# Token-major chunk data laid out by pair parity, PE transposes instead of identity products, and state and carried terms added on VectorE

## The chip, the cores and the metric

The kernel runs on 1 core of one Trainium2 chip. The metric is the device time of one execution, in microseconds (us); smaller is better. The median of three runs of the kernel before is 1719.84 us (1719.4 to 1721.35).

## What is computed

One step of a two-layer encoder trunk, for 64 tokens of a running stream and 512 tokens of a new one: 576 tokens, 9 chunks of 64. Per layer:

```
proj = RMSNorm(x) @ w_in                       # (576, 1024) @ (1024, 3344)
GLA group, 4 heads, 64 keys x 128 values, per chunk:
    scores = tril(q_e @ k_e^T);  o = scores @ v + q_e @ s
    s      = s * exp(last) + (k * exp(last - cum))^T @ v
RWKV-7 group, 8 heads of 64, per token:
    sa = s @ a;  s = s*w + outer(sa, b) + outer(v, k);  y = s @ r
x = x + [norm(o)*silu(g) | groupnorm(y)*g] @ w_out
x = x + ConvFFN(RMSNorm(x))                    # 1024 -> 2 x 2816 -> 1024
```

All in float32. The matmuls of the large projections run as three passes over operands split in two (high and low part, `fp32r`); those of the chunked recurrences are plain float32 products. The state of chunk 0 comes from the inputs, chunk 1 starts a new stream with a zero state, chunks 2 to 8 follow it.

## The kernel before, in words

Every engine has a program written out by hand, and semaphores join them. A list per engine (`PE_F`, `AC_B`, `DV_G` and so on, lines 106 to 132) names the events in the order in which the engine signals them, and a wait names an event of a chunk. So the order of the work is the order of the calls in each engine's loop, and nothing is rescheduled.

A layer has these stages: the projections (`dense`, L591 and L592), the chunked recurrences (the **scan stage**, L749 to L1088 on TensorE), the output projection and the ConvFFN. The change touches the scan stage alone. In it features lie on partitions: the 8 RWKV heads are 4 pairs `p`, with an even head on partitions 0 to 63 and an odd one on 64 to 127. X = A, B is a group of two pairs, `q` is the pair in its group, `hp` the head in its pair.

The loop `for i in range(-1, LAST)` (L998) does in one **step** the front of chunk j = i + 1 and the back of chunk i:

- `gram` (L760): per group 8 products with 128 columns (L770) and 4 with 64 (L773), of the chunk's keys and queries, into `gr[X]` and `tk[X]`. VectorE masks them (`mask_inverse` L1842, `mask_gram` L1852).
- `tokens` (L777): turns the three token-major operands (64 tokens on partitions), 12 products with `ident2` per group (L783). ScalarE copies them out (`copy_tokens`, L1335, 384 columns).
- `level` k = 1 to 5 (L787): powers and product of the triangular inverse. After each, ScalarE copies the powers (`copy_powers`, L1341), VectorE adds the product (`add_power`, L1859).
- `solve_z`, `solve_z1`, `solve_z2`, `solve_u` (L822 to L864): four products in a row with a copy between them: Z and Z1 go out on ScalarE (`copy_back`, L1350), W on VectorE (`add_rest`, L1871), U on ScalarE. `solve_z` accumulates the product with the state (L838) in PSUM.
- `outputs` (L866): y (L874, L877, L879) and the new state (L883, L886, L888), where L886 adds the old state as an identity product. VectorE scales the state (`new_state`, L1876), ScalarE copies y.
- `gla_scores`, `gla_tokens`, `gla_out`, `gla_state` (L897 to L950): the same for GLA; L949 adds the old state as an identity product.
- `post_means`, `post_squares_o`, `post_squares_y` (L957 to L986): at i = 0, 2, 4, 6, 7 the means for the normalisations; their logarithms and exponentials on ScalarE (L1386, L1392, L1398, L1404), scaling on VectorE (`scale_o` L1910, `scale_y` L1917).

Chunk 8's back stands after the loop (L1062 to L1085), and the output projection follows. In these products each head uses its own quarter of the PE array: an even head reads partitions 0 to 63 and writes 0 to 63, an odd one 64 to 127 both. Consecutive products alternate between these two tiles of 64x64:

```python
for p, h, q in heads(X):            # L782: h is the head's half of the partitions
    mm = e.matmul(tk[X][h, (2 * a + q) * C:(2 * a + q + 1) * C], src[h, p, :], ident2[h, :], ...)
```

Of the kernel before, what the change touches and what calls it, by code (L numbers as in the profile page):

```python
# [105 lines left out]
PE_F = ["gramA", "gramB", "tokA", "L1A", "tokB", "L1B", "L2A", "L2B", "L3A", "L3B", "L4A", "L4B", "L5A", "L5B"]  # L106
AC_F = ["tokA", "L1A", "tokB", "L1B", "L2A", "L2B", "L3A", "L3B", "L4A", "L4B"]
DV_F = ["EA", "DA", "EB", "DB", "MA", "MB", "L2A", "L2B", "L3A", "L3B", "L4A", "L4B", "L5A", "L5B"]
PO_F = ["TA", "TB"]

PE_B = ["Z", "Z1", "Z2", "U", "Y", "S"]
AC_B = ["Z", "Z1", "U", "Y"]
DV_B = ["W", "St"]
# [3 lines left out]
DV_G = ["scm", "Sg"]  # L117
# [17 lines left out]
def program(nc, x_prompt, x_sample, state_gla, state_rwkv, state_rwkv_shift, cache_ffn_conv,  # L135
# [4 lines left out]
    with ExitStack() as ctx:  # L140
# [66 lines left out]
        EK = [cut([P, NP, 2, P]) for _ in range(2)]  # L207
# [3 lines left out]
        Z, Z1, W, U = (cut([P, NP, C]) for _ in range(4))  # L211
        St = cut([P, NP, C])
        Sg = cut([P, 2, GDV])
        Sraw = cut([P, NP, C])
# [39 lines left out]
        zb, ys, gb, pb = bank(4), bank(5), bank(6), bank(7)  # L254
# [6 lines left out]
        def by_half(ap):  # L261
            return ap.rearrange("p (b t) -> p b t", t=HT)

# [200 lines left out]
        def _(po):  # L464
# [62 lines left out]
            for l in range(0, DEPTH):  # L527
# [10 lines left out]
                def start_inverse(j):  # L538

                    n = l * NCH + j  # L540
                    for X, N in ((0, "A"), (1, "B")):
                        po.wait_ge(dv_f, nth(DV_F, n, "E" + N))
                        e.tensor_tensor(DET[1][:, X, :, 1, :], DET[0][:, X, :, 0, :],
                                        ident2[:, :].unsqueeze(1).broadcast_to([P, 2, C]), ALU.add).then_inc(po_f, 1)
# [41 lines left out]
        def _(pe):  # L586
# [65 lines left out]
            for l in range(0, DEPTH):  # L652
# [96 lines left out]
                def heads(X):  # L749

                    for q in range(2):
                        for hp in range(2):
                            yield 2 * X + q, slice(64 * hp, 64 * hp + 64), q
# [6 lines left out]
                def gram(j, X):  # L760

                    N, cc = "AB"[X], bass.ds(j * C, C)
                    if j > 0:
                        front(dv_f, DV_F, j - 1, "L5" + N)
                    for q in range(2):
                        p = 2 * X + q
                        for b, src in ((0, KA[:, p, cc]), (1, R[:, 4 + p, cc])):
                            for hp in range(2):
                                h = slice(64 * hp, 64 * hp + 64)
                                e.matmul(gr[X][h, (2 * q + b) * P:(2 * q + b + 1) * P], src[h],  # L770
                                         RW[h, p:p + RT + 1:RT, cc], start=True, stop=True)
                    for p, h, q in heads(X):
                        mm = e.matmul(tk[X][h, 384 + q * C:384 + (q + 1) * C], KK[h, p, cc], KA[h, p, cc],  # L773
                                      start=True, stop=True)
                    mm.then_inc(pe_f, 1)

                def tokens(j, X):  # L777

                    cc = bass.ds(j * C, C)
                    front(dv_f, DV_F, j, "D" + "AB"[X])  # L780
                    for a, src in enumerate((KA[:, :, cc], R[:, 4:8, cc], R[:, 8:12, cc])):
                        for p, h, q in heads(X):  # L782
                            mm = e.matmul(tk[X][h, (2 * a + q) * C:(2 * a + q + 1) * C], src[h, p, :], ident2[h, :],  # L783
                                          start=True, stop=True)
                    mm.then_inc(pe_f, 1)

                def level(j, X, k):  # L787

                    N, d = "AB"[X], DET[(k + 1) % 2]
                    powers = gr[X][:, 0:4 * C].rearrange("p (q c t) -> p q c t", q=2, c=2)  # L790
                    product = pair3(tk[X][:, 0:2 * C])
# [8 lines left out]
                    for q in range(2):  # L800
                        for hp in range(2):
                            h = slice(64 * hp, 64 * hp + 64)
                            if k < 4:
                                mm = e.matmul(powers[h, q, 0], d[h, X, q, 2], d[h, X, q, 0], start=True, stop=True)  # L804
                        for hp in range(2):
                            h = slice(64 * hp, 64 * hp + 64)
                            if k < 5:
                                mm = e.matmul(powers[h, q, 1], d[h, X, q, 0], d[h, X, q, 2], start=True, stop=True)  # L808
                        for hp in range(2):
                            h = slice(64 * hp, 64 * hp + 64)  # L810
                            if k > 1:
                                mm = e.matmul(product[h, q], d[h, X, q, 2], d[h, X, q, 1], start=True, stop=True)  # L812
                    mm.then_inc(pe_f, 1)

                HEADS = (slice(0, C), slice(C, 2 * C))

                def pairs(out):

                    for p in range(NP):
                        yield p, p // 2, p % 2, out[:, p * C:(p + 1) * C]  # L820

                def solve_z(i):  # L822

                    cc = bass.ds(i * C, C)
                    front(ac_f, AC_F, i, "tokB")
                    front(dv_f, DV_F, i, "MB")
                    glas(ac_g, AC_G, i, "oE")
# [4 lines left out]
                    for p, X, q, o in pairs(zb):  # L832
                        for h in HEADS:
                            mm = e.matmul(o[h], EK[i % 2][h, p, 1, C:2 * C], tok[i % 2][h, X, 2, q, :],
                                          start=True, stop=i == 1)
                        if i != 1:
                            for h in HEADS:
                                mm = e.matmul(o[h], KK[h, p, cc], St[h, p, :], start=False, stop=True)  # L838
                    mm.then_inc(pe_b, 1)

                def solve_z1(i):

                    back(ac_b, AC_B, i, "Z")
                    front(dv_f, DV_F, i, "L5B")
                    for p, X, q, o in pairs(zb[:, 256:512]):
                        for h in HEADS:
                            mm = e.matmul(o[h], Tf[i % 2][h, p, :], Z[h, p, :], start=True, stop=True)  # L847
                    mm.then_inc(pe_b, 1)

                def solve_z2(i):  # L850

                    back(ac_b, AC_B, i, "Z1")
                    for p, X, q, o in pairs(zb):
                        for h in HEADS:
                            mm = e.matmul(o[h], EK[i % 2][h, p, 0, C:2 * C], Z1[h, p, :], start=True, stop=True)
                    mm.then_inc(pe_b, 1)

                def solve_u(i):

                    back(dv_b, DV_B, i, "W")  # L860
                    for p, X, q, o in pairs(zb[:, 256:512]):
                        for h in HEADS:
                            mm = e.matmul(o[h], Tf[i % 2][h, p, :], W[h, p, :], start=True, stop=True)  # L863
                    mm.then_inc(pe_b, 1)  # L864

                def outputs(i):  # L866

                    cc = bass.ds(i * C, C)
                    back(ac_b, AC_B, i, "U")
                    if i > 0:  # L870
                        back(ac_b, AC_B, i - 1, "Y")
                    for p, X, q, o in pairs(ys):
                        for h in HEADS:
                            e.matmul(o[h], tok[i % 2][h, X, 2, q, :], EK[i % 2][h, p, 1, 0:C], start=True, stop=False)  # L874
                        if i != 1:
                            for h in HEADS:
                                e.matmul(o[h], St[h, p, :], R[h, p, cc], start=False, stop=False)  # L877
                        for h in HEADS:
                            mm = e.matmul(o[h], U[h, p, :], EK[i % 2][h, p, 0, 0:C], start=False, stop=True)  # L879
                    mm.then_inc(pe_b, 1)  # L880
                    for p, X, q, o in pairs(ys[:, 256:512]):
                        for h in HEADS:
                            e.matmul(o[h], tok[i % 2][h, X, 1, q, :], tok[i % 2][h, X, 2, q, :], start=True, stop=False)  # L883
                        if i != 1:
                            for h in HEADS:
                                e.matmul(o[h], ident2[h, :], St[h, p, :], start=False, stop=False)  # L886
                        for h in HEADS:
                            mm = e.matmul(o[h], tok[i % 2][h, X, 0, q, :], U[h, p, :], start=False, stop=True)  # L888
# [8 lines left out]
                def gla_scores(j):  # L897

                    cc = bass.ds(j * C, C)
                    if j > 0:  # L900
                        glas(dv_g, DV_G, j - 1, "Sg")
# [18 lines left out]
                def gla_out(j):  # L920
# [3 lines left out]
                    if j > 0:  # L924
                        back(ac_b, AC_B, j - 1, "U")
# [13 lines left out]
                def gla_state(j):  # L939

                    glas(ac_g, AC_G, j, "oO")
                    for q in range(2):
                        o = gb[:, q * GDV:(q + 1) * GDV]
                        for h in HEADS:
                            mm = e.matmul(o[h], gtok[h, 256 + q * C:256 + (q + 1) * C], gtok[h, q * GDV:(q + 1) * GDV],
                                          start=True, stop=j == 1)
                        if j != 1:
                            for h in HEADS:
                                mm = e.matmul(o[h], ident2[h, :], Sg[h, q, :], start=False, stop=True)  # L949
# [7 lines left out]
                def post_means(g):  # L957
# [3 lines left out]
                    back(ac_b, AC_B, sum(GROUPS[g]) - 1, "Y")  # L961
# [1165 lines left out]
```

## Time and profile before

| | us |
|---|---|
| median of 3 runs | 1719.84 |
| the profiled execution, its own time | 1718.78 |
| its span | 1716.9 |
| PE busy | 1683.0 (98%), 19077 matmul records |
| DVE, ACT, POOL busy | 910.2, 665.4, 558.5 |
| scan stage, layer 0 and 1 | about 209.7 to 388.7 and 1050.2 to 1229 |

A plain float32 matmul leaves two load records and two matmul records in the trace, an `fp32r` one and a transpose one of each. A form such as "64*64 64x128" tells the rows and columns of the array that are used, then the moving operand. The end of a matmul is modelled, so a row's duration is latency; the pace is read from the starts of successive rows. The granted clock of TensorE is 0.997 of full speed over the span and 1.00 in the stages of the change.

### The profile page before, as it was taken

Reading aid. Unit: us, or ns where it says so; the run is one execution under the profiler, and the core shown is the slowest. Engines: PE = TensorE matmul, PEld = TensorE weight load, DVE = VectorE, ACT = ScalarE, POOL = GpSimd, SP = SyncE. Lnnn points to the kernel's source line nnn. Section 1 sums busy time; section 2 is a strip of 40 time slices with the busy share of each in tenths; the row PEclk is TensorE's granted clock in tenths of the full one; section 3 lists DMA queues with packets and bytes.
Section 4 is the critical chain, followed back from the end, with each engine's and each line's share of the span. In section 5 each row is a group of like instructions: output and inputs, shape, how many; then the busy total and the mean of one; then the engine's idle time right before and its main releaser. Section 6 shows DMA issues by size and latency. Waiting matters only on the chain.

```text
span 1716.9 us, 42320 instructions
## 1 busy us (share of the span) xinstructions
PE 1683.0 (98%) x19077; PEld 1626.7 (95%) x19077; DVE 910.2 (53%) x1382; ACT 665.4 (39%) x1017; POOL 558.5 (33%) x293
## 2 busy tenths in 40 slices
PE   7999999989999999999999999999899999999997
PEld 7999999879999999999999999998799999999997
DVE  4669534345566504666546883344456662166643
ACT  5444344554433212333343533454534331133323
POOL 5443301112343433334333432012134434343431
PEclk9999999999999999999999999999999999999999
DMA  5223200002222322223322222000022232222331
GB/s 147 63 74 84 69 24 4 4 3 68 76 85 86 98 76 75 87 86 96 83 75 74 74 74 58 10 4 3 20 83 79 86 96 85 71 83 87 92 94 56
DMA packets 218869, 115.51 MB, mean 67 GB/s; under 512 B 9332, under 2 KB 216450, under 8 KB 218690
## 3 DMA queue, kind: packets, MB, share of 16 engines
q1 hardware_dynamic: 218610, 112.79, 22.9%
q8 instruction: 151, 2.47, 0.6%
q14 instruction: 28, 0.23, 0.0%
q10 hardware_dynamic: 80, 0.02, 0.0%
HBM read 109.27 MB, written 3.53 MB: 66 GB/s over the span
## 4 chain that ended last, share of the span: by engine, by line
PE 95%; ACT 3%; DVE 1%; issue 0%; POOL 0%; DMA 0%; DVEq 0%; ACTq 0%
PE ps L591 37%; PE ps L592 37%; PE ps L808 2%; PE ps L812 2%; PE ps L770 2%; PE ps L804 1%; PE ps L783 1%; PE ps L596 1%; PE ps L914 1%; PE ps L874 1%; PE ps L977 1%; PE ps L706 1%; PE ps L931 1%; PE ps L863 1%; PE ps L847 0%; PE ps L888 0%
## 5 line engine op out<-in xcount | busy, mean ns | idle before, releaser
L518 POOL TENSOR_TENSOR wlo<-raw,whi 128x1024 fp32r<-128x1024 f32 (+1 forms) x188 | 508.7, 2706 | 865.1 <-ACT whi L1149 865.0
L1149 ACT ACTIVATE whi<-raw 128x1024 fp32r<-128x1024 f32 (+1 forms) x188 | 209.5, 1114 | 650.0 <-PE ps L592 650.0
L591 PE MATMUL ps<-xh,whi 128*128 128x288 f32 x1120 | 332.9, 297 | 4.2 <-DVE xl L1565 4.2
L592 PE MATMUL ps<-xh,whi 128*128 128x288 f32 x1120 | 331.2, 296 | 0.0
L591 PE MATMUL ps<-xl,whi 128*128 128x288 f32 x1120 | 330.3, 295 | 0.0
L592 PE MATMUL ps<-xl,whi 128*128 128x288 f32 x1120 | 329.0, 294 | 0.0
L591 PE MATMUL ps<-xh,wlo 128*128 128x288 f32 x1120 | 328.8, 294 | 0.0
L592 PE MATMUL ps<-xh,wlo 128*128 128x288 f32 x1120 | 328.7, 294 | 0.0
L591 PEld LDWEIGHTS ps<-xh,whi 128*128 128x128 f32 x1120 | 210.5, 188 | 6.3 <-issue 4.7
L592 PEld LDWEIGHTS ps<-xh,whi 128*128 128x128 f32 x1120 | 210.6, 188 | 0.2
L591 PEld LDWEIGHTS ps<-xh,wlo 128*128 128x128 f32 x1120 | 210.7, 188 | 0.0
L592 PEld LDWEIGHTS ps<-xl,whi 128*128 128x128 f32 x1120 | 210.6, 188 | 0.0
L591 PEld LDWEIGHTS ps<-xl,whi 128*128 128x128 f32 x1120 | 210.1, 188 | 0.0
L592 PEld LDWEIGHTS ps<-xh,wlo 128*128 128x128 f32 x1120 | 209.9, 187 | 0.0
L2035 DVE TENSOR_TENSOR x<-x,ps 128x576 f32<-128x576 f32 x48 | 36.2, 754 | 197.2 <-PE ps L592 197.2
L2073 DVE SCALAR_TENSOR_TENSOR cv<-up,par,cv 128x578 f32<-128x578 f32 x44 | 100.5, 2284 | 32.8 <-ACT cv L1521 32.8
L2088 DVE SCALAR_TENSOR_TENSOR hl<-hf,hh 128x576 fp32r<-128x576 f32 x44 | 98.4, 2237 | 33.3 <-ACT hh L1527 33.3
L592 PE MATMUL ps<-hh,whi 128*128 128x288 f32 x352 | 103.7, 295 | 0.0
L592 PE MATMUL ps<-hl,whi 128*128 128x288 f32 x352 | 103.6, 294 | 0.0
L591 PE MATMUL ps<-hl,whi 128*128 128x288 f32 x352 | 103.5, 294 | 0.0
L591 PE MATMUL ps<-hh,wlo 128*128 128x288 f32 x352 | 103.4, 294 | 0.0
L591 PE MATMUL ps<-hh,whi 128*128 128x288 f32 x352 | 103.4, 294 | 0.0
(294 smaller groups left out, 3286.7 us busy)
## 6 DMA issues: line engine op xcount, KB each, us to landing
raw<-in_ffn_w_up SPq DMA_DIRECT2D x88, 512.0 KB, 3.8
raw<-in_w_in SPq DMA_DIRECT2D x52, 512.0 KB, 3.7
raw<-in_ffn_w_down SPq DMA_DIRECT2D x32, 704.0 KB, 4.5
raw<-in_w_out SPq DMA_DIRECT2D x16, 512.0 KB, 3.6
xin<-in_x_prompt SPq DMA_DIRECT2D x4, 512.0 KB, 6.3
out<-xin SPq DMA_DIRECT2D x8, 256.0 KB, 2.9
out<-RW SPq DMA_DIRECT2D x16, 64.0 KB, 2.2
g<-in_rwkv_g SPq DMA_DIRECT2D x2, 256.0 KB, 3.0
```

The lines of the kernel that those rows point to most:

```text
L518: e.tensor_tensor(wlo[s][:, 0:width], raw[s][:, 0:width], whi[s][:, 0:width].bitcast(F32), ALU.subtract).then_inc(w_lo[s], 1)
L591: e.matmul(acc(out)[:, 0], lhsT, rhs[:, 0:HT], start=start, stop=stop)
L592: return e.matmul(acc(out)[:, 1], lhsT, rhs[:, HT:TOK], start=start, stop=stop)
L596: e.matmul(out[:, 0:512], lhsT, rhs[:, 0:512], start=True, stop=True)
L706: ws = e.matmul(PS[2][:, tt], w2a2[0:64, p * P:(p + 1) * P], R[0:64, 12, tt], start=True, stop=True)
L770: e.matmul(gr[X][h, (2 * q + b) * P:(2 * q + b + 1) * P], src[h], RW[h, p:p + RT + 1:RT, cc], start=True, stop=True)
L808: mm = e.matmul(powers[h, q, 1], d[h, X, q, 0], d[h, X, q, 2], start=True, stop=True)
L812: mm = e.matmul(product[h, q], d[h, X, q, 2], d[h, X, q, 1], start=True, stop=True)
L1149: e.activation(whi[s][:, 0:width], raw[s][:, 0:width], ACT.Copy).then_inc(w_hi[s], 1)
L2035: e.tensor_tensor(by_half(xt), by_half(xt), acc(PS[s]), ALU.add).then_inc(psum_free[s], 1)
L2073: e.scalar_tensor_tensor(out=cv[:, :], in0=up[:, 1:3 + TOK], scalar=par[:, cw + FF + f:cw + FF + f + 1], in1=cv[:, :], op0=ALU.mult, op1=A ...
L2088: e.scalar_tensor_tensor(out=hl[:, it, :], in0=hf[:, :], scalar=1.0, in1=hh[:, it, :].bitcast(F32), op0=ALU.mult, op1=ALU.subtract).then_i ...
```

## The change

Per chunk, the token-major data of a pair now lies on the partition half given by the parity of the pair (q), while the head parity (hp) picks the column block. `gram`, the product with the state (now `carried`) and `outputs` therefore read from one half and write to the other for half of their products: they use all four 64x64 tiles. `tokens` becomes 12 transposes of whole pairs, alternately 128 and 64 columns wide. The identity products of the states go. VectorE adds the old states, the carried part of Z and the carried part of y; ScalarE copies the two carried parts out of PSUM (`Zc`, `Yc`), VectorE writes Z and y in ScalarE's place. Both groups of a chunk are handled by one `gram`, one `tokens`, one copy of 768 columns. In the loop, `solve_z2` comes after `gla_scores` and the means, `solve_u` after both first levels, `outputs` after both second levels; ScalarE's `square_o` moves from the end of a step to the start of the next.

```diff
+                def gram(j):
...
                     if j > 0:
-                        front(dv_f, DV_F, j - 1, "L5" + N)
...
+                        front(dv_f, DV_F, j - 1, "L5B")
+                    if j > 0 and j != 2:
+                        back(ac_b, AC_B, j - 1, "Zc")
+                    for X in range(2):
+                        for b in range(2):
+                            at = (2 * X + b) * P
+                            for hp, q, p, own, tok_half in all_four(X):
+                                src = R[own, 4 + p, cc] if b else KA[own, p, cc]
+                                e.matmul(gr[hp][tok_half, at:at + P], src, RW[own, p:p + RT + 1:RT, cc], start=True, stop=True)
+                        for hp, q, p, own, tok_half in all_four(X):
+                            mm = e.matmul(tk[hp][tok_half, 384 + X * C:384 + (X + 1) * C], KK[own, p, cc], KA[own, p, cc],
...
+                def tokens(j):
...
+                    for a, first in enumerate((RT + NP, 4, 8)):
+                        for X in range(2):
+                            at, even, odd = a * P, first + 2 * X, first + 2 * X + 1
+                            e.transpose(tk[X][:, at:at + P], rows[:, bass.ds(odd * TOK + j * C - C, P)], ident[:, :])
+                            mm = e.transpose(tk[X][0:C, at:at + P], RW[:, even, cc], ident[:, :])
...
                         if k == 2:
                             front(po_f, PO_F, j, "T" + N)
+                            front(ac_f, AC_F, j, "tok")
...
+                def carried(i):
...
+                    front(ac_f, AC_F, i, "L4B")
...
+                        for hp, q, p, own, tok_half in all_four(X):
+                            mm = e.matmul(gr[hp][tok_half, X * C:(X + 1) * C], KK[own, p, cc], St[own, p, :],
...
+                def carried_y(i):
...
+                    glas(dv_g, DV_G, i, "Sa")
...
+                            mm = e.matmul(gb[h, p * C:(p + 1) * C], St[h, p, :], R[h, p, cc], start=True, stop=True)
...
                 def solve_z1(i):
 
-                    back(ac_b, AC_B, i, "Z")
+                    back(dv_b, DV_B, i, "Z")
...
                 def outputs(i):
...
+                    for X in range(2):
+                        for hp, q, p, own, tok_half in all_four(X):
+                            e.matmul(out_banks[own, q, X * C:(X + 1) * C], tok[i % 2][tok_half, X, 2, hp, :],
+                                     EK[i % 2][tok_half, hp, X, 1, 0:C], start=True, stop=False)
...
-                        if i != 1:
-                            for h in HEADS:
-                                e.matmul(o[h], ident2[h, :], St[h, p, :], start=False, stop=False)
...
-                        if j != 1:
-                            for h in HEADS:
-                                mm = e.matmul(o[h], ident2[h, :], Sg[h, q, :], start=False, stop=True)
...
+                def add_z(i):
+
+                    step(pe_b, PE_B, i, "Z")
...
+                        step(ac_b, AC_B, i, "Zc")
+                        e.tensor_tensor(Z[:, :, :], Zc[:, :, :], pair3(zb[:, 0:256]), ALU.add).then_inc(dv_b, 1)
...
+                        e.tensor_tensor(y, by_pair(Yc), from_rows(0), ALU.add).then_inc(dv_b, 1)
...
+                        e.tensor_tensor(by_pair(St), by_pair(St), from_rows(2 * C), ALU.add).then_inc(dv_b, 1)
+                        step(dv_b, DV_B, i, "Sa")
+                        e.tensor_tensor(St[:, :, :], St[:, :, :], decay, ALU.mult).then_inc(dv_b, 1)
...
                 scale_y(N_Y - 1)
+                add_z(LAST)
                 add_rest(LAST)
```

The last hunks are VectorE's: `add_z`, `add_y`, `new_state` (`new_gla_state` changes in the same way) and its order after the loop. In its loop the order is now `add_z(i)`, `mask_inverse(j)`, `mask_gram(j, 0)`, `mask_gram(j, 1)`, `add_rest(i)`, and `new_state(i)`, `add_y(i)` follow the adds of level 2. For chunk 1, whose state is zero, nothing is carried.

`all_four(X)` yields, for hp and q in 0, 1, the pair p = 2X + q, its rows `own` = half hp and the half `tok_half` = half q.

## Rows read from the trace of the kernel before

**Rows 1.** The page: the chain that ended last, by engine.

```profile
PE 95%; ACT 3%; DVE 1%; issue 0%; POOL 0%; DMA 0%; DVEq 0%; ACTq 0%
```

**Rows 2.** Busy time in layer 0's scan stage: window, us, PE, PEld, DVE, ACT, POOL, clock, DMA.

```profile
209.70:385.70 176.00, 170.71 (x4535) 155.89 (x4534) 71.67 (x204) 88.00 (x203) 21.14 (x29) 1.00 0.05 12
```

**Rows 3.** Groups of instructions by line, PE: form, records, busy us, mean ns, idle before.

```profile
L770 PE MATMUL ps<-RW 64*64 64x128 f32 x576 | 37.8, 270 | 0.0
L783 PE MATMUL ps<-ident,RW 64*64 64x64 f32 x864 | 32.0, 219 | 0.0
...
L883 PE MATMUL ps<-work 64*64 64x64 f32 x288 | 20.1, 218 | 0.0
...
L886 PE MATMUL ps<-work,ident 64*64 64x64 f32 x256 | 18.1, 218 | 0.0
...
L838 PE MATMUL ps<-work,RW 64*64 64x64 f32 x256 | 15.8, 218 | 0.0
...
L773 PE MATMUL ps<-RW 64*64 64x64 f32 x288 | 14.5, 218 | 0.0
...
L949 PE MATMUL ps<-work,ident 64*64 64x128 f32 x128 | 12.3, 269 | 0.0
```

**Rows 4.** Timeline of PE in the step i = 2: start us, latency us, line, records.

```profile
257.68 1.04 PE L770 MATMUL ps<-RW 64*64 64x128 f32 x16
258.55 0.40 PE L773 MATMUL ps<-RW 64*64 64x64 f32 x8
258.78 0.63 PE L847 MATMUL ps<-work 64*64 64x64 f32 x16
...
269.92 0.28 PE L812 MATMUL ps<-work 64*64 64x64 f32 x4
270.13 0.66 PE L914 MATMUL ps<-ident,G 128*64 128x128 f32 x8
270.72 0.45 PE L916 MATMUL ps<-ident,G 64*64 64x64 f32 x8
```

**Rows 5.** Timeline of PE where it transposes, between projections.

```profile
798.87 0.27 PE L1114 MATMUL ps<-ident,last_rows 128*28 128x128 f32 x1
798.98 0.27 PE L1115 MATMUL ps<-ident,last_conv 128*88 128x128 f32 x1
...
1691.33 1.91 PE L643 MATMUL ps<-ident,work 128*128 128x128 f32 x16
1693.00 0.38 PE L591 MATMUL ps<-hh,whi 128*128 128x288 f32 x1
```

**Rows 6.** Timeline of PE, products from the two halves of the partitions.

```profile
49.24 0.69 PE L706 MATMUL ps<-RW,w2a 64*128 64x512 f32 x1
49.24 0.69 PE L707 MATMUL ps<-RW,w2a 64*128 64x512 f32 x1
49.77 0.59 PE L706 MATMUL ps<-RW,w2a 64*128 64x512 f32 x1
```

**Rows 7.** Timeline of ACT and DVE from step i = 4 to 5; last, a group by line.

```profile
316.69 0.36 ACT L1353 ACTIVATE work<-ps 128x256 f32<-128x256 f32 x1
...
316.97 2.17 DVE L1922 SCALAR_TENSOR_TENSOR RW<-RW,par,work 128x128 f32<-128x128 f32 x4
319.06 0.28 DVE L1847 TENSOR_TENSOR work<-ps,m_be 128x128 f32<-128x128 f32 x1
...
L1338 ACT ACTIVATE work<-ps 128x384 f32<-128x384 f32 x18 | 8.8, 491 | 26.0 <-PE ps L783 26.0
```

**Rows 8.** Timeline of PE and DVE after the loop, layer 0; idle before in brackets.

```profile
377.76 0.68 PE L847 MATMUL ps<-work 64*64 64x64 f32 x16
...
378.93 0.68 PE L855 MATMUL ps<-work 64*64 64x64 f32 x16 [0.48 <-ACT work L1353]
...
380.32 0.41 DVE L1874 TENSOR_TENSOR work<-work,ps 128x256 f32<-128x256 f32 x1
...
380.78 0.68 PE L863 MATMUL ps<-work 64*64 64x64 f32 x16 [1.17 <-DVE work L1874]
```

More of the change, by code:

```diff
@@ L205, in cut @@
                                    **dict(zip(names[1:], sizes[1:])))
[L207 removed]
+        EK = [cut([P, 2, 2, 2, P]) for _ in range(2)]
         tok = [cut([P, 2, 3, 2, C]) for _ in range(2)]
@@ L211, in program @@
         Z, Z1, W, U = (cut([P, NP, C]) for _ in range(4))
+        Sraw = W
+        Zc, Yc = (cut([P, NP, C]) for _ in range(2))
         St = cut([P, NP, C])
         Sg = cut([P, 2, GDV])
-        Sraw = cut([P, NP, C])
         gtok = cut([P, 2 * GDV + 2 * C])
@@ L758, in _ @@
                 back = glas = front
-                def gram(j, X):
-                    N, cc = "AB"[X], bass.ds(j * C, C)
+                def gram(j):
+                    cc = bass.ds(j * C, C)
                     if j > 0:
-                        front(dv_f, DV_F, j - 1, "L5" + N)
[L765 to L775, printed above, removed]
@@ L792, in level @@
+                def level(j, hp, k):
+                    N, d = "AB"[hp], DET[(k + 1) % 2]
+                    powers = gr[hp][:, 0:4 * C].rearrange("p (x c t) -> p x c t", x=2, c=2)
+                    product = pair3(tk[hp][:, 0:2 * C])
                     if k == 1:
@@ new lines, in solve_z @@
+                def solve_z(i):
+                    front(ac_f, AC_F, i, "tok")
+                    front(dv_f, DV_F, i, "MB")
+                    glas(ac_g, AC_G, i, "oE")
+                    if i > 0:
+                        back(dv_b, DV_B, i - 1, "Y")
+                    for n, hp, X, o in solved(zb):
+                        for h in HEADS:
+                            mm = e.matmul(o[h], EK[i % 2][h, hp, X, 1, C:2 * C], tok[i % 2][h, X, 2, hp, :],
+                                          start=True, stop=True)
+                    mm.then_inc(pe_b, 2 if i == 1 else 1)
@@ L1063, in _ @@
                 squares = SQ[:, 0, :].rearrange("p (a t) -> p a t", t=2 * C)
+                carried(LAST)
                 solve_z(LAST)
-                back(ac_b, AC_B, LAST - 1, "Y")
-                glas(dv_g, DV_G, LAST, "Sg")
-                chunk_mean(7, gb[:, 0:256], R[:, 0:4, seventh])
+                front(dv_f, DV_F, LAST, "L5A")
+                back(dv_b, DV_B, LAST - 1, "Y")
+                chunk_mean(7, bank(2)[:, 0:256], R[:, 0:4, seventh])
+                carried_y(LAST)
                 solve_z1(LAST)
@@ L1975, in _ @@
                         add_power(j, 1, k)
+                        if k == 2 and i >= 0:
+                            new_state(i)
+                            add_y(i)
                     if i == LAST - 1:
@@ L2007, in _ @@
                 new_state(LAST)
+                add_y(LAST)
                 cc = group(N_Y)[1]
```

289 lines of the change are left out of this document (156 added, 133 removed).

## The prediction

> **What bounds the kernel now.** First the chain of waits: TensorE holds 95% of it [rows 1]. Then the busy time of the scan stage, the only one that the change touches: PE is busy for 170.7 of 176.0 us at the full clock of 2.4 GHz, ACT for 88, DVE for 72 [rows 2]. So a product that leaves PE shortens the stage, as long as ScalarE and VectorE deliver in time. Last the pace of PE, from starts. Eight products of 128 columns (16 records, L770) take 258.55 - 257.68 = 0.87 us, 0.218 for a pair; four of 64 columns (L773) take 0.23, 0.117 for a pair [rows 4]. A "pair" is what now shares the array: an even head and an odd one. There are 18 chunks (9 in each layer); a float32 product is two records.
>
> **What leaves PE.** `tokens` loses all of L783: 864 records, 216 pairs, x 0.117 = 25.2 us. The identity products of the RWKV state (L886) are 256 records, 64 pairs, 7.5 us; those of the GLA state (L949) 128 records, 32 pairs x 0.218 = 7.0 us [rows 3, 4].
>
> **What comes: the transposes.** 12 x 18 = 216. Sixteen of them started within 1693.00 - 1691.33 = 1.67 us, 0.104 each, and one after another of another width 0.11 later [rows 5]. I take 0.11, for the narrow ones too, since there 28 columns cost no less: 23.8 us. They use all 128 rows, the products around them 64. Such an excursion has a row: L914 starts 0.21 after the last L812 group, 0.09 more than its pace, and its four products take 0.59 where two pairs take 0.44, 0.15 more [rows 4]. That makes 0.24; I take 0.34, as an estimate for wide loads, x 18 = 6.1 us. So the "one-pass" transposes save nothing: 29.9 us for 25.2, +4.7. The balance of PE so far is -14.5 + 4.7 = -9.8 us.
>
> **What may shrink: the crossed products.** `gram`, `carried` and `outputs` keep their counts, but reach all four 64x64 tiles, in the order (rows 0, columns 0), (0, 1), (1, 0), (1, 1) or likewise. Does the array run four at once? No row has four 64x64 tiles; two rows bound it. L914 runs two products on all rows into different columns: four of them, 128 columns each, in 0.59 us, where one at a time they would need 4 x 0.218 = 0.87 [rows 4]. L706 and L707 read different halves of the rows into the same columns, start together and follow each other every 0.53 us with 512 columns [rows 6], so they overlap too. The change also puts the two row halves into different banks of PSUM, as L706 and L707 do. If both overlaps combine, four take the time of two. Half of L770 (144 pairs x 0.218 = 31.4) is 15.7 us; half of L773, L838 and the four lines of `outputs` like L883 (72 + 64 + 288 = 424 pairs x 0.117 = 49.6) is 24.8 us [rows 3, 4]. The bounds are 0 and 40.5 us; below 0 if products from the same rows don't overlap (a rival). I take 40.5, since each of the two overlaps has its row. PE: -50.3 us.
>
> The Trainium skill, "TensorEngine Tiling (Array Packing)", sections on tiling modes and restrictions, speaks for this: 64x64 mode has four independent tiles, and row tiles need different banks. No trace here shows all four.
>
> **What comes back as waits**, per layer, with durations of [rows 7, 8] and the paces above, found by laying out the calls of the four engines' loops in their written order, one after the other, before and after the change; PE comes earlier to nearly every wait.
> - z1 to z2: from the last z1 product through ScalarE's copy to z2 took 0.70 us, 0.48 of it idle [rows 8]. `gram` of group B lay between them; now `gla_scores` alone does (0.23), and the means where there are any. Chunks 0, 1, 3, 5: 4 x 0.41 = 1.6 us.
> - `add_z` stands before z1 and `gram` is short: three waits of about 0.4, 1.2 us.
> - After steps 2, 4 and 6: ScalarE is in its logarithms and exponentials and reaches the copy of Z at 316.69 only [rows 7]. Before, the first half of `gram` ran meanwhile; now `gram` itself waits for that copy (`Zc` reads its banks): 1.3 + 1.7 + 1.7. VectorE's scaling of y ends at 319.06, where the masks start [rows 7]; `add_z` queues behind it, and z1 waits 1.2 + 1.0 + 1.0 more. Less the 0.8 of waits that are there today: 7.0 us. This is the largest term.
> - Chunk 0: the transposes wait for both masks (0.8), level 2 for the copy of 768 columns (0.5; 384 take 0.49 and 256 take 0.36 [rows 7], so about 0.85), less what goes: 1.3 us.
> - After the loop, `add_z(LAST)` stands behind four scalings, so at 380.3 [rows 8], where z1 started at 377.76: z1 waits 3.5, z2 and u 0.6 each, the means of chunk 8 1.5 (three VectorE operations where there was one and a copy), with 0.4 more in small waits; today's waits there are 4.1. So +2.6 us.
>
> Sum 13.7 per layer, 27.4 for both. The copies of Yc, the second state operation and `add_y` (about 0.4 us each on an engine that is busy for 41%) lie beside `gla_tokens` and level 3, over 1.5 us of PE; their cover gone, they would cost 1.2 us a chunk. POOL's start of the inverse waits for one mask of both groups, 0.15 us later, long before level 2. SP's queue and the DMAs are not passed by anything that moves.
>
> **Sum**: -50.3 + 27.4 = -22.9 us. The profiled execution took 1718.8, 1.1 below the median; 1719.8 - 22.9 = **1697 us**. Own range of this case 1688 to 1706: the waits may be 18 to 36 us.
>
> **Rivals.**
> - *PE is fed no faster.* Today's best pace is one record in 29 ns (0.23 us for 8, L773 [rows 4]). If that is the sequencer's limit, four passes of 64 columns need 0.117, as now, and only `gram`'s 128 columns gain: -9.8 - 15.7 = -25.5, waits +21: 1715 us. Against it: 0.117 also is what a pair's array time asks for. Chance 0.17.
> - *Two at a time.* The crossed tiles only pair. PE -9.8, and with `gram` at full length fewer waits, about 17: 1727 us. Against it stand both rows above. Chance 0.17.
> - *The transposes pay for each change of width* (the other side, with its place and price). They alternate 128 and 64 columns, 11 changes within a chunk, 198 in all. A change between 64*64 and 128*64 costs 0.09 + 0.15, so 0.12 to 0.24 each way [rows 4]; at 0.18, 36 us: 1733 us. It decides from 0.116 us a change (22.9 / 198). Against it: L1114 (28 columns) to L1115 (88) took 0.11, the pace without any change [rows 5]. Chance 0.12.
> - *Products from the same rows don't overlap*: the crossed ones take twice as long, 1719.8 - 9.8 + 81 + 14 = 1805 us; L914 speaks against it. Chance 0.03.
>
> The Trainium skill, same page, "Key Properties", says that a change of tiling mode drains TensorE, and its restrictions bar transposes of float32 from column tiling; by that the third rival's 1733 us would come out. The trace agrees for 64*64 to 128*64, not for L1114 to L1115.
> For the first rival, "TensorE: Matmul & The Clock Gate", Part 1, gives 25 ns as the smallest distance of two starts; four passes of 64 columns would then need 100 ns, a seventh of 49.6 us would go, and an estimate by that page is 1709 us. No trace here shows it.
>
> **Numbers.** Forecast 0.47, rivals 0.17, 0.17, 0.12, 0.03; 0.04 is left for a mixture. About 0.2% (3.4 us) can be told from no change: faster is below 1716.4, slower above 1723.3. Faster: 0.47 + 0.12 of the first rival + 0.03: 0.62. Same: 0.05 of the first, 0.04 of the second, 0.02: 0.11. Slower: 0.27. Range 1690 to 1737: it takes in three of the cases and leaves out the fourth rival, some of the third and the low end of the forecast.
>
> **What would show it.** Four records of L770's successor starting within some 20 ns and `gram` at some 1.1 us instead of 2.2; transposes 0.11 apart whatever their width; after steps 2, 4, 6 PE waiting for ScalarE's copy of Zc, then for `add_z`; after the loop z1 waiting 3 us or more for VectorE. If `gram` still takes over 2 us, the forecast is wrong by its main term; if the 12 transposes take over 2.5 us, by the second.

## The result: about half of the forecast gain, and the profile after

The kernel after takes **1708.48 us** by the median of four runs (1708.15 to 1712.2), the kernel before, beside it, 1719.99. The ratio is 0.9937 (95% interval 0.992 to 0.9954): faster by 11.5 us, by more than the 3.4 us that can be told from no change. Forecast was 1697 us, 22.9 less. The sign is right and the wide range (1690 to 1737) holds the time, but half of the gain is missing, and the forecast's own range, 1688 to 1706, is missed by 2.5 us.

| | before | after |
|---|---|---|
| profiled execution, us | 1718.78 | 1708.42 |
| its span, us | 1716.9 | 1706.6 |
| granted clock over the span | 0.997 | 0.987 |
| scan stage, layer 0 / 1, us | 179.5 / 179.5 | 172.8 / 175.2 |
| matmul records | 19077 | 18045 |

The page of the kernel after, busy time and the chain by engine, answers to [rows 1]:

```profile
PE 1650.7 (97%) x18045; PEld 1583.9 (93%) x18045; DVE 932.9 (55%) x1414; ACT 659.0 (39%) x995; POOL 557.7 (33%) x293
...
PE 92%; ACT 3%; DVE 3%; issue 1%; DMA 1%; POOL 0%; SPq 0%; DVEq 0%; ACTq 0%
```

TensorE still holds the chain, VectorE has gone from 1 to 3%. From here on a scan stage is measured from the first product of `gram` to the last of `turn_state`, which turns the final state. Busy time in such windows has the columns of [rows 2]. First the kernel before, both layers:

```profile
209.66:389.16 179.50, 173.32 (x4560) 157.88 (x4560) 73.65 (x210) 91.19 (x208) 21.14 (x29) 1.00 0.05 12
1049.54:1229.04 179.50, 173.32 (x4560) 157.88 (x4560) 73.60 (x210) 91.20 (x208) 21.14 (x29) 1.00 0.05 12
```

Then the kernel after, both layers, and five short stretches inside them:

```profile
210.26:383.05 172.79, 155.34 (x4044) 135.24 (x4044) 84.95 (x226) 87.84 (x197) 20.99 (x29) 0.96 0.05 12
1043.42:1218.65 175.23, 157.43 (x4043) 137.00 (x4044) 85.53 (x226) 87.82 (x197) 20.96 (x29) 0.94 0.05 12
...
303.60:310.40 6.80, 4.94 (x160) 4.63 (x158) 4.23 (x10) 4.55 (x10) 1.27 (x1) 1.00 0.01 2
310.40:317.20 6.80, 5.93 (x63) 5.04 (x64) 3.24 (x9) 0.87 (x2) 3.27 (x4) 0.50 0.01 2
317.20:324.00 6.80, 6.80 (x234) 6.49 (x232) 2.34 (x7) 3.50 (x9) 0.00 (x0) 1.00 0.02 5
371.80:378.60 6.80, 5.80 (x106) 4.65 (x110) 2.32 (x4) 3.35 (x6) 0.00 (x0) 0.50 0.01 2
...
1204.70:1218.30 13.60, 10.05 (x128) 7.89 (x130) 7.14 (x19) 4.36 (x9) 0.00 (x0) 0.50 0.00 1
```

Two things are to be seen. Both layers do the same work, before in the same time, after in times 2.4 us apart. And the clock column, 1.00 before, is 0.96 and 0.94: for 6.8 us in step i = 5, for 6.8 us after the loop of layer 0 and for 13.6 us at the end of layer 1 TensorE is granted half its clock, 1.2 instead of 2.4 GHz. (Two more of 3.4 us each lie in layer 1, at about 1109 and 1146.6.) No step of the forecast has this. The page's row of tenths over 40 slices doesn't show it: it says 9 nearly throughout.

**The four tiles** do what was forecast. The timeline of PE, DVE and ACT in the kernel after, from step i = 4 to 5 (start us, latency us):

```profile
308.38 0.36 ACT L1386 ACTIVATE work<-ps 128x256 f32<-128x256 f32 x1
...
308.65 2.17 DVE L1999 SCALAR_TENSOR_TENSOR RW<-RW,par,work 128x128 f32<-128x128 f32 x4
...
308.89 0.67 PE L784 MATMUL ps<-RW 64*64 64x128 f32 x16 [1.68 <-ACT work L1386]
...
309.35 0.32 PE L786 MATMUL ps<-RW 64*64 64x64 f32 x8
...
309.46 0.65 PE L784 MATMUL ps<-RW 64*64 64x128 f32 x16
...
309.90 0.32 PE L786 MATMUL ps<-RW 64*64 64x64 f32 x8
...
310.75 0.41 DVE L1919 TENSOR_TENSOR work<-work,ps 128x256 f32<-128x256 f32 x1
...
311.21 1.12 PE L878 MATMUL ps<-work 64*64 64x64 f32 x16 [0.99 <-DVE work L1919]
```

Sixteen records of 128 columns now take 0.46 us (308.89 to 309.35) and eight of 64 columns 0.11, where one group took 0.87 and 0.23 [rows 4]. The whole `gram` takes 1.1 us. The lines around them are the two waits that were forecast: `gram` waits 1.68 us for the copy of Z (`Zc`, L1386), z1 (L878) then 0.99 us for `add_z` (L1919), which stands behind four scalings (L1999).

**The transposes** keep one pace whatever their width: 0.17 us after the first, then 0.11 from start to start. PE of the kernel after, one chunk:

```profile
228.02 0.33 PE L797 MATMUL ps<-ident,RW 128*128 128x128 f32 x1
228.19 0.27 PE L798 MATMUL ps<-ident,RW 128*64 128x128 f32 x1
228.30 0.27 PE L797 MATMUL ps<-ident,RW 128*128 128x128 f32 x1
...
229.28 0.27 PE L798 MATMUL ps<-ident,RW 128*64 128x128 f32 x1
229.48 0.33 PE L818 MATMUL ps<-work 64*64 64x64 f32 x4
```

**After the loop**, layer 0, kernel after, what answers to [rows 8]:

```profile
371.26 0.41 DVE L1919 TENSOR_TENSOR work<-work,ps 128x256 f32<-128x256 f32 x1
...
371.73 1.08 PE L878 MATMUL ps<-work 64*64 64x64 f32 x16 [2.94 <-DVE work L1919]
...
373.29 1.12 PE L886 MATMUL ps<-work 64*64 64x64 f32 x16 [0.48 <-ACT work L1398]
...
374.93 1.12 PE L894 MATMUL ps<-work 64*64 64x64 f32 x16 [0.53 <-DVE work L1935]
```

z1 waits 2.94 us. And its own sixteen records last 1.08 us where the same shape took 0.68 before [rows 8]: this is at half clock (0.50 in the window 371.80 to 378.60 above).

### The profile page after: what moved, and what is told of

It is laid out like the page before. It is cut to its first block, busy times and chain, and to the rows that moved or that the text cites. A ratio compares the mean times of both kernels' runs of the same rounds, so it can differ in the third digit from the quotient of the medians.

```text
span 1706.6 us, 40374 instructions
## 1 busy us (share of the span) xinstructions
PE 1650.7 (97%) x18045; PEld 1583.9 (93%) x18045; DVE 932.9 (55%) x1414; ACT 659.0 (39%) x995; POOL 557.7 (33%) x293
## 4 chain that ended last, share of the span: by engine, by line
PE 92%; ACT 3%; DVE 3%; issue 1%; DMA 1%; POOL 0%; SPq 0%; DVEq 0%; ACTq 0%
PE ps L601 37%; PE ps L602 37%; PE ps L821 2%; PE ps L818 2%; PE ps L824 2%; PE ps L606 1%; PE ps L797 1%; PE ps L886 1%; DVE RW L1999 1%; PE ps L878 1%; ACT L1443 1%; PE ps L798 1%; PE ps L942 1%; PE ps L1003 1%; PE ps L894 1%
## 5 line engine op out<-in xcount | busy, mean ns | idle before, releaser
L1910 DVE TENSOR_TENSOR work<-work,ps 128x128 f32<-128x128 f32 x144 | 39.6, 286 | 123.0 <-PE ps L824 123.0
L602 PE MATMUL ps<-hh,whi 128*128 128x288 f32 x352 | 103.7, 295 | 0.0
```

The lines of the kernel that those rows point to most:

```text
L602: return e.matmul(acc(out)[:, 1], lhsT, rhs[:, HT:TOK], start=start, stop=stop)
L1910: e.tensor_tensor(dst, DET[(k + 1) % 2][:, X, :, 1, :], src, ALU.add).then_inc(dv_f, 1)
```

## The experiments

The theory, A: the forecast of the instructions and waits holds, and what is missing is the clock. TensorE's granted clock falls to half behind the new waits, and the stretches at half cost some 11 us. The rival, B: the waits alone cost more than laid out, and the clock changes nothing that bounds. Each kernel ran beside the kernel before on the same chip. In the table "gain" is the median of before less that of the kernel; clock is that of the profiled execution over its whole span.

| kernel | median us | ratio to before (95%) | gain | clock |
|---|---|---|---|---|
| after | 1708.48 | 0.9937 (0.992 to 0.9954) | 11.5 | 0.987 |
| after, again | 1708.2 | 0.9923 (0.991 to 0.9936) | 12.2 | 0.988 |
| waits filled | 1699.13 | 0.987 (0.9856 to 0.9883) | 21.6 | 0.996 |
| last wait filled | 1704.48 | 0.9898 (0.9881 to 0.9914) | 16.2 | 0.998 |
| filled twice over | 1710.07 | 0.9939 (0.9926 to 0.9953) | 10.3 | 0.996 |
| order in the loop | 1696.54 | 0.9864 (0.9849 to 0.9879) | 23.8 | 0.992 |
| order after the loop | 1706.18 | 0.9906 (0.989 to 0.9922) | 14.5 | 0.991 |
| both orders | 1692.02 | 0.9836 (0.9823 to 0.9849) | 28.9 | 0.992 |
| two tiles | 1729.3 | 1.0052 (1.0037 to 1.0067) | -8.4 | 0.987 |
| crossed identity products | 1695.41 | 0.9854 (0.9837 to 0.9871) | 25.5 | 0.988 |
| crossed, both orders | 1681.8 | 0.977 (0.9754 to 0.9785) | 38.9 | 0.991 |
| the same, waits filled | 1678.9 | 0.9756 (0.9743 to 0.9769) | 41.5 | 0.996 |

**Work for nothing in the waits.** The added products go into a bank that is free then, and nothing reads them. If A holds, added work makes the kernel faster.

```diff
+FILL = {3: (2, 2), 5: (3, 2), 7: (3, 2)}
...
+                def fill(i, n):
+                    t = tok[i % 2]
+                    for k in range(n):
+                        for h in HEADS:
+                            e.matmul(out_banks[h, 1, 0:256], t[h, 0, 0, 0, :], t[h, 0, 0:2], start=True, stop=True)
...
+                    if i in FILL:
+                        fill(i, FILL[i][0])
                     gram(j)
+                    if i in FILL:
+                        fill(i, FILL[i][1])
...
                 carried_y(LAST)
+                fill(LAST, 6)
                 solve_z1(LAST)
```

> The kernel after, plus work for nothing in the waits of the scan: pairs of 64x64 products of 256 columns into the free second bank of the outputs (0.107 us a pair at the full clock), two or three pairs before the crossed products and two before z1 in steps 3, 5 and 7, six pairs after the loop before z1. That is 20 pairs a layer, 4.3 us of added TensorE work in both layers, nothing taken away. Theory A (the forecast's missing half is the clock: behind the new waits TensorE's granted clock falls to half in the scan stages, which costs some 12 us): fewer half-clock stretches in the scan, and the time falls to 1697 to 1704 although work was added. Theory B (the new waits themselves are longer than forecast, the clock changes nothing that bounds): the time stays at 1708.5 or rises by up to 4.3 us, to 1713.

Measured 1699.13 us, in A's range and 9.3 below the kernel after. Its timeline of PE in front of `gram` of step i = 5, and the two scan stages:

```profile
309.70 1.49 PE L865 MATMUL ps<-work 64*64 64x256 f32 x12
311.54 0.67 PE L785 MATMUL ps<-RW 64*64 64x128 f32 x16 [0.34 <-ACT work L1399]
...
211.98:380.85 168.87, 159.73 (x4125) 136.60 (x4124) 85.12 (x226) 87.87 (x197) 21.03 (x29) 1.00 0.05 13
1041.25:1210.36 169.11, 159.68 (x4124) 136.37 (x4124) 84.97 (x226) 87.87 (x197) 21.03 (x29) 1.00 0.05 13
```

The clock is 1.00 in both stages, and they are 3.9 and 6.1 us shorter than in the kernel after, with the same products, the same waits for the same events and 160 records more. B, by which the clock is worth nothing, allowed no gain at all: it falls. One number of the expectation was wrong. A product of 256 columns is two records that follow each other every 0.1 us (the starts of 12 records fill about 309.70 to 310.8), so a pair costs 0.4 us, not 0.107, and the added work was some 16 us for both layers. It was nearly hidden because the waits had room for its 8 us a layer. From the start of the last record before each wait to the start of the first one behind it they are 1.47 + 1.13 + 1.90 + 1.21 + 1.90 + 1.21 + 3.16 = 12.0 us.

**Only the wait after the loop filled** (the last `fill` alone).

> Only the six pairs of products for nothing after the loop, before z1 (0.64 us a layer at the full clock, inside the wait of 3.16 us). Theory A (the clock falls behind the waits after the loop and stays at half through z2, u and the last outputs): less of the half-clock stretch after the loop, 1703 to 1707. Theory B (that stretch waits for ScalarE and VectorE, so TensorE's clock is worth nothing there): 1708 to 1709.

Measured 1704.48 us (1699.14 to 1705.95), in A's range. The profiled execution was one of the two fast ones, 1700.90 us. It has no half-clock stretch in either scan stage, though the waits within the loop are the same to 0.1 us, so for the loop the edit can't be the reason. It therefore shows the stage of the kernel after at full clock:

```profile
212.31:380.47 168.16, 152.84 (x4069) 132.49 (x4068) 84.98 (x226) 87.87 (x197) 21.00 (x29) 1.00 0.05 13
1040.87:1211.11 170.24, 153.76 (x4069) 133.00 (x4068) 85.04 (x226) 87.88 (x197) 21.01 (x29) 1.00 0.05 13
```

Layer 1 has one gap of about 1.5 us inside `gram` of step i = 0 that the kernel after doesn't have and that nothing here explains.

**The control**, the kernel after once more.

> The kernel after, unchanged, once more, as the control beside the others of this group. 1708 to 1711 by the median. Theory A (the clock's falls behind the waits come and go from one execution to the next): single executions differ by several us, down to 1703, and the half-clock stretches lie elsewhere than in the first profile, while the waits themselves are the same to 0.1 us. Theory B (the waits alone): executions within 2 us of each other and the same steps long.

Measured 1708.2 us by the median, single executions from 1704.13 to 1710.15. The half-clock stretches lie in part elsewhere: within layer 0's loop the first profile has one from 310.4 to 317.2 us, this one two of 3.4 us, at 310.6 and at 348.1. In layer 1 the one at 1109 stays and the one at 1146.6 is gone. The waits are the same in both (1.68 us for `gram`, 0.99 for z1 in step i = 5). So one step can be compared with itself. Windows of step i = 5, where the three kernels have the same instructions and waits. First the kernel after:

```profile
308.89:327.20 18.31, 17.26 (x441) 15.84 (x442) 9.06 (x25) 6.80 (x18) 4.54 (x5) 0.81 0.01 4
1144.29:1161.33 17.04, 15.99 (x441) 14.90 (x443) 8.95 (x25) 6.70 (x18) 4.53 (x5) 0.90 0.02 5
```

The control:

```profile
308.20:325.49 17.29, 16.25 (x441) 15.15 (x444) 8.98 (x25) 6.70 (x18) 4.54 (x5) 0.90 0.02 4
1144.14:1160.04 15.90, 14.66 (x443) 13.74 (x445) 8.96 (x25) 6.70 (x18) 4.55 (x5) 1.00 0.02 5
```

The kernel with only the last wait filled:

```profile
310.78:326.61 15.83, 14.58 (x442) 13.67 (x444) 8.98 (x25) 6.71 (x18) 4.56 (x5) 1.00 0.01 3
```

The step's length goes by the clock column alone: 15.8 to 15.9 us at 1.00, 17.0 to 17.3 with 3.4 us at half, 18.3 with 6.8 us. A microsecond at half clock costs 0.34 to 0.42 us here. Together with the filled waits this shows the cause.

The scatter of single executions alone would not: the two fastest here have the highest clock (1704.13 and 1705.64 us at 0.991, the others 0.987 to 0.989), but the kernel before also ran from 1718.54 to 1724.16 us in one group of nine, with clocks of 0.995 to 0.997.

**Twice the work for nothing.**

> The kernel after with twice the work for nothing (40 pairs a layer, 8.6 us in both instead of 4.3; before the crossed products, before z1 and after the loop). Theory A: once the clock stays at full, more of it wins nothing and what doesn't fit into the waits costs, up to 4.3 us more than with the single amount (1699.1): 1699 to 1704. Theory B (it was something else in the added products, as their writes or their order): the gain doubles, 1690.

Measured 1710.07 us, above both theories. The clock is 1.00 in both stages, so A's part on the clock holds; its range, 1699 to 1704, didn't, as it was reckoned with 0.107 us a pair. PE in front of the same `gram`:

```profile
309.88 2.54 PE L865 MATMUL ps<-work 64*64 64x256 f32 x21
312.05 0.33 PE L785 MATMUL ps<-RW 64*64 64x128 f32 x2
```

No wait is left, and the products for nothing hold `gram` back: it starts 2.17 us after the first of them instead of 1.84. The stages are 5.7 and 6.9 us longer than with the single amount. The clock at full is worth only what the filled time doesn't take.

**The order of ScalarE, VectorE and GpSimd**, which shortens the waits instead of filling them.

```diff
+LATE = (2, 4, 6)
...
                         copy_carried_y(i)
+                        if i - 1 in LATE:
+                            rstd_y(Y_AT[i - 1])
...
+                    if i - 1 in LATE:
+                        scale_y(Y_AT[i - 1])
                     if py is not None:
                         centre(py)
...
-                scale_y(N_Y - 1)
                 add_z(LAST)
+                scale_y(N_Y - 1)
```

> Only the order on ScalarE, VectorE and GpSimd changes: after steps 2, 4 and 6 the scaling of the finished outputs (its exp, its product, its last part) goes behind the next step's carried shares, and after the loop the states are added before that scaling. TensorE's work is untouched; the waits for Zc and for the added states after steps 2, 4 and 6 and z1's wait after the loop get shorter by some 1 to 2 us each. Theory A (waits plus the clock that falls behind them): 12 us by the waits alone and up to 12 more as the half-clock stretches go: 1685 to 1697. Theory B (the clock costs nothing): 1696 to 1699. Theory C (TensorE then meets the next wait at once, and those waits are not what bounds): 1704 to 1709.

Measured 1692.02 us, within A's range and below B's. PE in step i = 5:

```profile
306.18 0.67 PE L787 MATMUL ps<-RW 64*64 64x128 f32 x16 [1.16 <-ACT work L1389]
...
307.31 0.68 PE L881 MATMUL ps<-work 64*64 64x64 f32 x16
...
209.59:373.84 164.25, 152.04 (x4045) 132.52 (x4044) 82.45 (x226) 88.08 (x198) 20.98 (x29) 0.98 0.05 13
1035.00:1202.17 167.17, 153.80 (x4045) 133.90 (x4044) 82.51 (x226) 87.74 (x197) 20.98 (x29) 0.97 0.05 13
```

`gram` waits 1.16 instead of 1.68 us, z1 not at all, and step i = 5 takes 14.61 us instead of 18.31 (15.83 at full clock). What is left at half clock lies after the loop. The gain over the kernel after is 28.9 - 11.85 (the mean of its two rows) = 17.0. The part within the loop alone:

> Of the changed order only the part after steps 2, 4 and 6 (scaling of the finished outputs behind the next step's carried shares); the order after the loop is as in the kernel after. Both together took 17 us off the kernel after, the part after the loop alone 3.7. If they add: 1696. Theory A (the falls of the clock also have a share): a half-clock stretch stays after the loop in both layers, none within the loop; 1694 to 1698. Theory B (after the loop is all that matters, as it holds the longest wait): 1704 to 1709.

Measured 1696.54 us: A's range, and its half-clock stretches are after the loop alone (10.2 and 6.8 us). The part after the loop alone:

> One change of order: after the loop VectorE adds the states before it scales the outputs of the last group but one, so that z1 waits less. Theory A (wait and clock): the wait of 3.16 us before z1 falls by 1 to 1.8 us a layer, and the stretch at half clock behind it shortens, 1699 to 1704. Theory B (wait alone): 3.6 us off by my layout of the engines' loops, 1705. Theory C (the scaling is then late for what comes next after the loop): 1707 to 1709.

Measured 1706.18 us, with single runs in two groups (1701.53 and 1701.93; 1706.18 to 1707.88). z1's wait fell by 1.05 us a layer as meant. That lies between C and B, and A's range is missed: the interval of the ratio overlaps that of the kernel after, so this part alone can't be told from nothing. Its profiled execution shows why it scatters: layer 0 took 173.18 us with clock 0.95, layer 1, the same work, 167.52 with 1.00.

**Two tiles instead of four**, the same products in another order.

```diff
...
-                    for X in range(2):
-                        for hp, q, p, own, tok_half in all_four(X):
...
+                    for side in range(2):
+                        for X in range(2):
+                            for hp, q, p, own, tok_half in from_rows_of(X, side):
...
```

> Same products, other order: in the crossed products, the carried ones and the outputs those that share rows of the array (or a bank) are issued in runs of two tiles, so that only two tiles are in use at once. Theory A (four tiles run side by side at full rate): these three groups cost what two tiles at a time cost, about 40 us more for both layers of TensorE time, of which waits take some back: 1727 to 1742. Theory B (the gain on TensorE's own work is not from four tiles but from elsewhere, the removed products or the transposes): 1707 to 1712.

Measured 1729.3 us, A's range and slower than the kernel before. So the change's gain stands on the four tiles: without them, it loses. The two stages, then the first and the last row of one chunk's `outputs`, which holds 64 records in both kernels:

```profile
209.93:392.27 182.34, 167.88 (x4044) 148.52 (x4044) 85.77 (x226) 88.16 (x198) 21.00 (x29) 0.97 0.05 12
1053.51:1236.36 182.85, 168.22 (x4045) 148.71 (x4044) 85.70 (x226) 88.18 (x198) 21.03 (x29) 0.97 0.05 12
...
249.66 0.27 PE L913 MATMUL ps<-work 64*64 64x64 f32 x1
...
251.35 0.28 PE L924 MATMUL ps<-work 64*64 64x64 f32 x4
```

The corresponding rows of one chunk with four tiles, in the kernel with only the last wait filled:

```profile
375.21 0.34 PE L910 MATMUL ps<-work 64*64 64x64 f32 x8
...
376.08 0.30 PE L921 MATMUL ps<-work 64*64 64x64 f32 x8
```

With two tiles 60 records start in 1.69 us, one in 28 ns; with four 56 start in 0.87 us, one in 16 ns.

**Crossed identity products instead of the transposes.** The token-major tile `tok` is laid out to fit; its readers change their indices, which the excerpt leaves out.

```diff
...
-                            e.transpose(tk[X][:, at:at + P], rows[:, bass.ds(odd * TOK + j * C - C, P)], ident[:, :])
-                            mm = e.transpose(tk[X][0:C, at:at + P], RW[:, even, cc], ident[:, :])
+                            for hp, q, p, own, tok_half in all_four(X):
+                                mm = e.matmul(tk[hp][tok_half, (2 * a + X) * C:(2 * a + X + 1) * C], src[own, p, :],
+                                              ident2[own, :], start=True, stop=True)
...
```

> The twelve transposes of a chunk become 24 crossed identity products of 64x64, four tiles at once, and the token-major tile is laid out by the parity half alone. Theory A (a transpose costs 0.109 us whatever its width, four crossed products cost 0.058 us together): a chunk's tokens go from 1.31 to 0.35 us, 0.96 us a chunk, 17 us for both layers; what the waits and the clock take of it stays open, so 1690 to 1703. Theory B (TensorE already waits for the other engines in these steps, more speed there only lengthens the waits and the half-clock stretches): 1705 to 1711.

Measured 1695.41 us, A's range. The timeline of PE:

```profile
228.03 0.87 PE L797 MATMUL ps<-ident,RW 64*64 64x64 f32 x46
228.73 0.28 PE L818 MATMUL ps<-work 64*64 64x64 f32 x4
```

From 227.92, where its first records start, to 228.73 the 48 records take 0.81 us. The expectation had 0.35: it forgot that a plain product is two records. Against 1.46 us for the twelve transposes (228.02 to 229.48) this saves 0.65 us a chunk, 11.7 us in all. By the gains it is 25.5 - 11.85 = 13.6; where the clock falls differs as well.

**Both together.**

> The crossed identity products for the tokens together with the changed order on ScalarE, VectorE and GpSimd. Alone they took 13.1 and 16.5 us off the kernel after. If the two are independent: 1679. Theory A (the waits let the clock fall; with fewer waits the faster tokens pay in full, 17 us): 1672 to 1677. Theory B (with less TensorE work the waits that the order took away come back): 1683 to 1690.

Measured 1681.8 us. The two add nearly (1679), and neither A's nor B's range holds it. The stages took 162.0 and 162.2 us with clock 0.97, so the clock falls there too. **With the waits filled as well:**

> The fastest so far (crossed identity products and changed order, 1681.8) plus work for nothing in what waits are left: two pairs of products before the crossed products of steps 3, 5 and 7, four pairs after the loop, 2.1 us of added TensorE work in both layers. Theory A (half-clock stretches are left there too, in the profile 10.2 us after the loop in both layers and longer steps 2 and 7): 1675 to 1680. Theory B (nothing left to win): 1681.8 to 1684.

Measured 1678.9 us, as A has it. Its scan stages, both at full clock:

```profile
212.32:371.67 159.35, 148.22 (x4408) 128.81 (x4408) 81.84 (x226) 86.88 (x197) 21.01 (x29) 1.00 0.06 14
1032.08:1189.50 157.42, 147.72 (x4409) 128.43 (x4408) 82.00 (x226) 86.90 (x197) 20.99 (x29) 1.00 0.06 14
```

Both of these versions beat the kernel before and the kernel after. The second's interval (0.9743 to 0.9769) overlaps the first's (0.9754 to 0.9785), and they ran on different chips, so its lead of 3 us is likely, not shown.

## Why the prediction was half right

- **The step that failed** is "What comes back as waits": it priced the new waits by their own length, at the full clock, as the stage had it in [rows 2]. What these waits do to the clock was put at nothing, without a reason. In the kernel after the clock falls behind those waits, by 6.8 + 6.8 us in layer 0 and 3.4 + 3.4 + 13.7 in layer 1, 34 us in all. The cost: the stages took 172.8 and 175.2 us, at full clock one takes 168.16, so (172.8 - 168.16) + (175.2 - 168.16) = 11.7 us, against the 11.4 that are missing from the forecast. With 170.24 for layer 1, the other full-clock stage (its unexplained gap of 1.5 us included), it is 9.6. So it is 10 to 12 us, and the match to 0.3 us is closer than the data allow.
- **The rest of the sum held** to about 2 us. At full clock a stage went from 179.5 to 168.16, 11.34 us; for two layers 22.7 (20.6 with 170.24 for layer 1), forecast 22.9. The signs that the prediction named for its success came true while half of the gain was missing (`gram` at 1.1 us, the transposes 0.11 apart, the waits in their places): all were about instructions and waits, none about the clock.
- *Crossed products, -40.5 us*: right as far as it was measured. `gram` took 1.1 us instead of 2.2, the records of `outputs` start 16 ns apart instead of 28; `carried` was not measured by itself. Giving up two of the four tiles cost 8.4 + 11.85 = 20.3 us although TensorE then waited less.
- *Transposes*: 0.109 each, as taken. The excursion was put at 0.34 us; it is 1.46 - 12 x 0.109 = 0.15, so 3.4 us less. It didn't show in the sum, so something else took as much; that wasn't traced.
- *Waits*: the gap in front of z1 after the loop was put at 3.5 us, it is 3.16 between starts (2.94 idle); `gram`'s after steps 2, 4, 6 at 1.3, 1.7, 1.7, found 1.47, 1.90, 1.90 between starts; z1's at 1.2, 1.0, 1.0, found 1.13, 1.21, 1.21. All named in the right places. The windows show the sum as well: span less PE busy is 6.2 us in a stage before and 17.4 and 17.8 after, so 11.3 and 11.6 more, where 13.7 were laid out. Busy time counts the latency of the last product before a wait, so the two aren't the same measure, but the 5.7 us a layer that are missing can't lie in longer waits. That speaks against B too.
- **The rivals.** That PE is fed no faster than a record in 29 ns falls: 46 records of 64 columns start within 0.70 us, one in 15 ns. Two at a time falls with it. That transposes pay for a change of width falls with the pace of 0.11. That products from the same rows don't overlap falls too. None of them was the reason, though the measured time lies between the forecast and the first of them (1715): a total near a rival's is no evidence for it.
- The Trainium skill, "TensorE: Matmul & The Clock Gate", Part 1, has the clock as something that TensorE's recent activity releases, throttled otherwise. The trace agrees: the stretches at 1.2 GHz follow the waits, and go when all of these are filled; within the loop they also went when the waits there were shortened. The prediction drew on that page for the distance of two starts (25 ns for one engine) and not for this. By that figure it had 1709 us, near the measured time for a reason that the trace excludes: records into four tiles follow each other every 15 ns on the average.
- The same skill, "TensorEngine Tiling (Array Packing)", restrictions, bars float32 transposes from column tiling, and its Key Properties let a change of tiling mode drain the engine. Here float32 transposes of 128*128 and 128*64 alternate 0.11 us apart and show neither a bar nor a stop. If the narrow ones count as column tiling, the trace differs from the page, and the trace decides; whether they do, no run shows. Between the 64*64 products and the transposes, where the mode does change, the way there and back costs 0.15 us a chunk.

Left open: what makes the clock fall behind a wait in one execution and not in the next. The waits before it were the same to 0.1 us in executions with and without a fall.

## What to carry to other kernels

When a change takes work from TensorE and leaves waits of one to three microseconds, compare the granted clock stage by stage before and after: here 24 us of waits (12 a layer) brought another 10 to 12 us by the clock, as much as the whole gain that was left. Shorten such waits by the order of the other engines first; where that ends, products for nothing into a free bank can pay, up to the length of the wait and no further. And compare the same step between layers and between executions: the same instructions in 15.8 and 18.3 us point at the clock, not at the program.

## What the runs showed of the hardware

- Products in four different 64x64 tiles run side by side, at nearly twice the rate of two: 48 records of 64 columns took 0.81 us, an average of 17 ns from record to record, where two tiles take one record in 29 ns [rows 4].
- TensorE's clock fell to half inside a stage that it is busy for 90% of, and where it does differs between executions of one kernel: step i = 5 took 15.9, 17.0, 17.3 and 18.3 us with the same instructions and waits, at clocks of 1.00, 0.90, 0.90 and 0.81.
- More work made the kernel faster: some 16 us of products whose results nothing reads won 9.3 us; twice as much won nothing.
- A stretch at 1.2 GHz doesn't cost half of its length: 0.34 to 0.42 us per us. That TensorE waits in a part of it anyway is the likely reason; it wasn't tested.
